# Attention on TensorE: a head's score products are issued one head earlier, and VectorE's softmax is written as two steps

## The reference

```python
def attention(q, k, v):
    s = jnp.einsum('bqhgd,bkhd->bhgqk', q, k, preferred_element_type=jnp.float32) * (HEAD_DIM ** -0.5)
    p = jax.nn.softmax(s, axis=-1).astype(v.dtype)
    return jnp.einsum('bhgqk,bkhd->bqhgd', p, v)
...
    k_all = jnp.concatenate([kc, kl], axis=1)
    v_all = jnp.concatenate([vc, vl], axis=1)
    ol = blocked_attention(ql.reshape(B, T, KV_HEADS, GROUP, HEAD_DIM), k_all, v_all)
    yl = (ol.reshape(B, T, ATT_W) * jax.nn.silu(gl)) @ w_out
```

## Time and profile before

| what | value |
|---|---|
| median of the runs shown (3 runs) | 3914.93 us |
| their lowest and highest | 3911.76 and 3934.26 us |
| the profiled execution: its span | 3915.0 us |
| TensorE busy, share of the span | 92% |
| VectorE, ScalarE, GpSimd | 52%, 39%, 6% |
| mean granted TensorE clock of the core | 0.965 |

### The profile page before, as it was taken

One profiled execution on the slowest core, in us unless ns is written; L12 is line 12 of the kernel. 1 busy time (PEld: TensorE's weight loads), 2 busy tenths in 40 slices (PEclk: granted clock), 3 DMA queues, 4 the chain that ended last, 5 costly groups with the idle time before them and its releaser, 6 DMA issues. The chain is left out here.

```text
span 3915.0 us, 73945 instructions
## 1 busy us (share of the span) xinstructions
PE 3610.4 (92%) x32796; PEld 2969.4 (76%) x32796; DVE 2019.5 (52%) x3476; ACT 1544.0 (39%) x2599; POOL 251.1 (6%) x295
## 2 busy tenths in 40 slices
PE   7899999999899998989988799989999999999998
PEld 3577666767666676777678689847989799999877
DVE  1444454544445457675465646666544455555444
ACT  1333343333333333354454444334443444444433
POOL 0001111110111113002000000100000000000000
PEclk8899899999999998999999899999999999999999
DMA  9423333242343315443324454424554545555554
GB/s 365 145 74 96 89 106 104 81 126 70 94 126 91 100 56 192 170 153 106 97 97 138 154 166 143 138 97 140 172 183 140 169 163 183 183 179 189 194 174 160
DMA packets 349484, 548.76 MB, mean 140 GB/s; under 512 B 11724, under 2 KB 119916, under 8 KB 346988
## 3 DMA queue, kind: packets, MB, share of 16 engines
q1 hardware_dynamic: 346716, 538.78, 42.6%
q10 hardware_dynamic: 2448, 5.24, 0.4%
HBM read 535.86 MB, written 8.13 MB: 139 GB/s over the span
## 5 line engine op out<-in xcount | busy, mean ns | idle before, releaser
L302 PE MATMUL lane<-r,r 128*128 128x256 f32 (+1 forms) x8520 | 1504.7, 325 | 48.4 <-DVE r L260 41.7
L302 PE MATMUL bank<-r,r 128*128 128x512 f32 (+2 forms) x6360 | 1403.0, 359 | 37.6 <-DVE r L260 29.0
L302 PEld LDWEIGHTS lane<-r,r 128*128 128x128 f32 x8520 | 1260.6, 190 | 222.2 <-DVE r L260 48.6
L260 DVE TENSOR_TENSOR r<-ring,r 128x1024 fp32r<-128x1024 f32 x770 | 939.6, 1227 | 940.9 <-ACT r L299 939.6
L302 PEld LDWEIGHTS bank<-r,r 128*128 128x128 f32 x6360 | 1045.0, 193 | 253.5 <-issue 55.3
L299 ACT ACTIVATE r<-ring 128x1024 fp32r<-128x1024 f32 x770 | 807.9, 1055 | 967.5 <-PE lane L302 566.7
L302 PE MATMUL lane<-arena 64*64 64x64 f32 (+5 forms) x13708 | 664.2, 250 | 57.1 <-issue 20.4
L302 PEld LDWEIGHTS lane<-arena 64*64 64x64 f32 (+3 forms) x13708 | 504.9, 140 | 203.3 <-issue 121.4
L299 ACT ACTIVATE arena<-lane 128x256 f32<-128x256 f32 (+3 forms) x578 | 252.6, 457 | 567.0 <-PE lane L302 468.0
L271 DVE COPY arena<-lane 128x256 f32<-128x256 f32 (+3 forms) x366 | 131.7, 361 | 303.5 <-PE lane L302 300.5
L260 DVE TENSOR_TENSOR arena<-arena 128x256 f32<-128x256 f32 (+7 forms) x568 | 259.8, 488 | 36.0 <-ACT arena L299 14.8
(11 more groups left out here) (95 smaller groups left out, 1357.5 us busy)
## 6 DMA issues: line engine op xcount, KB each, us to landing
ring<-in_w_gate_up SPq DMA_DIRECT2D x88, 1024.0 KB, 5.1
ring<-in_mod_w SPq DMA_DIRECT2D x73, 1024.0 KB, 5.3
ring<-in_ev_w_in SPq DMA_DIRECT2D x44, 1024.0 KB, 8.7
ring<-in_w_down SPq DMA_DIRECT2D x44, 1024.0 KB, 5.1
ring<-in_od_w_in SPq DMA_DIRECT2D x40, 1024.0 KB, 5.1
ring<-in_w_in SPq DMA_DIRECT2D x40, 1024.0 KB, 5.1
ring<-in_w_xkv SPq DMA_DIRECT2D x32, 1024.0 KB, 5.2
ring<-in_ev_w_out SPq DMA_DIRECT2D x28, 1024.0 KB, 5.1
```

The lines of the kernel that those rows point to most:

```text
L260: return Nothing() if self.e is None else self.e.tensor_tensor(o, a, b, op)
L302: return Nothing() if self.e is None else self.e.matmul(o, l, r, start=start, stop=stop)
```

## The change

It has three parts. In `attend`, the scores of head h + 1 are issued ahead of the probability transposes of head h, where they were issued after the values of head h; the first head of the stage, and a head whose queries are not transposed yet (head 12), still issue their own. On VectorE, `soft_rows` is taken apart for this attention: the step `scores` does both rows' maxima, and a new step `soften` waits for the exponentials and does both reciprocals and scalings. `soften` of head h + 1 stands behind `p_turned` of head h, mostly with a weight unit between it and the maxima. VectorE's own wait for `pS_read` goes; the one on ScalarE stays.

```diff
+    scored = set()
+
+    def score(h):
+        if h < 16 and h // 4 in ready and h not in scored:
+            scored.add(h)
+            for qt in range(2):
+                step("scores", h // 4, h, qt, bank(aux))
+
+    def soften(h):
+        if h in scored and h not in softened:
+            softened.add(h)
+            step("soften", h)
...
     def attend(n):
         for h in range(4 * n, 4 * n + 4):
-            for qt in range(2):
-                step("scores", n, h, qt, bank(aux))
+            if h not in scored:
+                score(h)
+                yield ATT[0]
+            soften(h)
+            score(h + 1)
             yield ATT[0]
             for kt2 in range(2):
                 step("p_turned", h, kt2, bank(aux))
+            soften(h + 1)
             yield ATT[1]
             step("values", n, h, bank(aux))
             yield ATT[2]
...
     def scores(n, h, qt, b):
         i = (2 * h + qt) % 4
-        if h >= 2:
-            v.wait_ge(*at("pS_read", h - 2))
-        soft_rows(b, 512, M.pS[i], float(P) ** -0.5, M.st1[:, 32 + 4 * i:36 + 4 * i], ("pS", h, qt))
+        st = M.st1[:, 32 + 4 * i:36 + 4 * i]
+        full(b)
+        v.maximum(st[:, 0:1], M.bank[b[0]]).then_inc(*v.n())
+        own()
+        v.ts(st[:, 1:2], st[:, 0:1], -float(P) ** -0.5, None, MUL).then_inc(*v.n(("top", "pS", h, qt)))
+
+    def soften(h):
+        for qt in range(2):
+            i = (2 * h + qt) % 4
+            st = M.st1[:, 32 + 4 * i:36 + 4 * i]
+            v.wait_ge(*at("exp", "pS", h, qt))
+            v.recip(st[:, 3:4], st[:, 2:3]).then_inc(*v.n())
+            own()
+            v.ts(M.pS[i], M.pS[i], st[:, 3:4], None, MUL).then_inc(*v.n(("pS", h, qt)))
```

More of the change, by code:

```diff
@@ L1161, in order_of_work @@
     ready = set()
+    scored = set()
[8 more added lines that the diff above has]
+            step("soften", h)
+    softened = set()
     def attend(n):
         for h in range(4 * n, 4 * n + 4):
-            for qt in range(2):
-                step("scores", n, h, qt, bank(aux))
+            if h not in scored:
[3 more added lines that the diff above has]
+            score(h + 1)
             yield ATT[0]
@@ L3010, in vector_program @@
         read_out, combine, first_done, split_w, split, pool, pool_mix, pool_done, gate_diag, add_first, ctx_done,
-        norm0, norm0_q, h1, h1_done, to_q, to_k, to_v, k_rows, v_rows, q_rows, hn_square, hn_gain, hn_turn, hn_turned, hn_done, scores,
+        norm0, norm0_q, h1, h1_done, to_q, to_k, to_v, k_rows, v_rows, q_rows, hn_square, hn_gain, hn_turn, hn_turned, hn_done, scores, soften,
         values, gate_heads, add_second, attended, norm1, rms, rms_turned, vg_in, gla_ready, gl_gate, gl_decay, gl_spread, gl_keys,
```

## The result

Measured: 3897.43 us in the median (6 runs, 3884.12 to 3903.27) against 3916.14 of the kernel before beside it (6 runs), ratio 0.9945 with a 95% interval from 0.9929 to 0.9961. The change takes 18.7 us away where 10 were forecast. 3897.43 lies in the range, but not in the part of it that carried the forecast (3899 to 3911): it lies where the prediction put the case without a fall of the clock (3890 to 3899).

The account below looks back on a forecast made before the run. TensorE was taken as the bound, with 26 idle us in attention's 223. Idle time falls 13.6 us, less 3.2 for the clock, making 10.4: 3915.0 to 3905 us, range 3896 to 3917 (main case 3899 to 3911).

Parts of the forecast that it names:

- the case without a fall of the clock: Rival: TensorE's clock stays up in attention, giving 3895.5 us; range 3890 to 3899, chance 0.14.
- short waits and `values`, gone: Away from the gate groups, transposes' waits for VectorE's scaling and one `values` wait for ScalarE vanish: 16.8 us saved.
- A: End of gate group 0, with head 10: 5.4 us lost before and after, nothing gained.
- B: End of gate group 1 and head 12: loss goes from 6.1 to 7.5 us, 1.4 worse.
- C: End of gate group 2: no attention step covers the wait, 2.6 us lost becomes 4.1, 1.5 worse.
- clock, before and after: TensorE's granted clock in attention: falls cost 5.9 us before and 9 after, three at 3 each.
- head 0: First head: VectorE still has its scalings ahead of head 1's maxima, costing 0.3 us.
- Part one: Heads away from the gate groups: transposes find their scalings ready, saving 16.8 us together with a wait of `values`.
- Part three: TensorE's clock falls behind three long waits at gate-group ends, 3 us each: 9 against 5.9, 3 us worse.
- The bank coupling: Rival: a head's second transposing waits for the next head's exponentials, 1.9 us to spare; 3925 us, chance 0.07.
- The worse long waits: Rival: at gate-group ends, falls cost 5 us each and another transposing stalls 2; 3913 us, chance 0.16.
- nothing gained: Rival: TensorE's waits count only if units behind can't make up for them; 3915 us, chance 0.05.

Follow-up runs that it names:

- e2: Kernel before with the split softmax alone (both maxima, then both scalings), TensorE's order unchanged: 3893.13 us, ratio 0.9937.
- e3: Changed kernel with 28 extra 128x256 matmuls filling the long wait at the start of gate groups 1 to 3: 3896.49 us, ratio 0.9948.
- e1: Changed kernel with TensorE's new order but VectorE's softmax in one piece as before: 3900.32 us, ratio 0.9961.
- e8: Changed kernel with three extra VectorE reductions ahead of the first maximum at heads 3 to 7 and 9: 3920.24 us, one run.
- e7: Changed kernel with one extra VectorE reduction ahead of the first maximum at heads 3 to 7 and 9: 3895.41 us, one run.
- e9: Kernel of e2 with one extra VectorE reduction ahead of the first maximum at heads 3 to 7 and 9: 3906.99 us, one run.
- e4: Changed kernel with the gate's tiles reordered (four tanh before the high parts, eight products before the low parts): 3886.79 us, ratio 0.9920.
- e5: Kernel of e2 with the gate's tiles reordered as in e4: 3887.02 us, ratio 0.9918.

## Why the prediction was wrong

By the starts on TensorE the losses of the stage are, forecast and measured, in us:

| term | forecast | measured |
|---|---|---|
| short waits and `values`, gone | 16.8 | 15.6 |
| A, idle, before and after | 5.4, 5.4 | 5.4, 4.4 |
| B, the same | 6.1, 7.5 | 6.1, 5.5 |
| C, the same | 2.6, 4.1 | 2.6, 3.5 |
| clock, before and after | 5.9, 9 | 5.7, 4.8 |
| head 0 | +0.3 | 0 |
| sum of the change | -10.4 | -17.2 |

The last line of the measured column is worked out from those above it, 15.6 + 14.1 - 13.4 + 5.7 - 4.8, and comes within 0.3 of the stage's 17.5. The prediction's own sum takes 3.2 for the clock where its terms, 9 less 5.9, give 3.1.

- **Part one, the short waits: right.** They were on the path, they go, nothing takes their place, and head 0 costs nothing (0.3 forecast). The 1.2 us too much are mostly that a wide unit behind scores takes 3.21 us from start to start (1889.66 to 1892.87) and not 2.88, in a quiet order as well. So the 0.48 us that the prediction booked as lost overlap behind each wide unit was mostly the length of the unit itself: what an interruption costs beyond its wait is 0.15 (4.61 less 3.21 less 1.25). What I left out is that the split alone does it too (e2), so the chain that I named as the cause has two ends, and the change cuts both.
- **The places A, B and C: the long waits right, what follows them wrong.** Forecast 4.7, 4.2 and 4.1 lost, measured 4.4, 3.8 and 3.5; at A the release came as forecast, and TensorE was ready at S + 5.33 and not S + 5.0, for the same 3.2 us of the unit behind scores. Then I added 0.7 for `values`, 0.9 for the diagonals and 2.4 for head 12's transposes. The first two aren't there, and the third is 1.6, 1.2 ahead of the transposes and 0.4 within them. These were computed with TensorE at full clock, and the next part put the same stretch at half clock. TensorE can't be slow and also early. e3 shows it: at full clock the waits of `values`, diagonals and transposes appear, 0.51, 0.79 and 1.56 us, and the distance over B stays 11.70 against 11.69.
- **Part three, the failing step: "I take 3 us for each of the three".** The fall comes, and it costs 1.6 each. I took the size from one stretch behind 4.40 us without work at another place of the program and put what follows on top by guess, while three falls that the stage before shows cost 1.7, 2.4 and 1.6. The 9 against 4.8 us are 4.2 of the 7.1 us between forecast and stage; the follow-on waits and the shorter long waits are 3.6 more, part one takes 1.2 back, and 0.5 are small terms. The 5.9 us that the prediction itself had for three falls of today, 2 us each, spoke against the 3.
- **The rivals.** That the clock doesn't fall is refuted as a mechanism, though its 3895.5 lies nearer to the result than my forecast, which is luck: it left out 4.8 us of falls, and had 2.7 us too much in the waits. The bank coupling exists, with the slack that I gave it, and isn't reached: no such wait appears at the heads away from the gate groups. The worse long waits didn't come, and "nothing gained" neither. Of the signs, only one of the three long waits is over 4 us (4.11, 3.27, 3.36), and TensorE's idle time in the stage fell to 11.9 us and not to 17.

The Trainium skill, "TensorE: Matmul & The Clock Gate", section "HAM oscillation — how this bites in real kernels", says that each long enough gap is paid with a cold start; the trace agrees, with half clock behind all three and 1.6 us each. It didn't weigh against the change in the end: ten short waits were worth some 13 us, and of the 4.8 us of the three falls only some 2.3 would have come back with the clock kept up (0.81 at A, nothing at B, 1.52 at C, by e3).

## What to carry to other kernels

Charge a slower clock and the waits behind it once, not twice: lay out the time that each engine arrives with the clock in it, and take the larger. When a consumer waits for a chain that goes back and forth between two engines, first ask whether the chain can be issued in two passes (maxima, then scalings), for that alone gave all of the gain here, and moving the consumer away as well added nothing (2 us less in the stage, nothing that shows in the whole time). A further prize was next door: doing the operations that free a bank ahead of those that don't was worth 7 to 10 us of the stage in every order of the rest, and 2.6 behind it.

## What the runs showed of the hardware

- Over the twelve traces here, TensorE's waits in this stage of 3.2 us and more (17 of them) were followed by a fall to half clock within the next 2 us in 15 cases; two of 3.36 us were not (in e1 and e8). Of 18 waits from 1.9 to 2.7 us, 12 were, and the same length went both ways at the same place of the program: 2.20 and 2.21 us. Of 40 waits from 0.9 to 1.8 us, one was (1.56 in e3). The same page's section "A second HAM failure mode: psum-queue depth-cycling" names short idles between groups as a cause of falls; ten waits of 1.0 to 1.3 us in the kernel before, each with 1.00 behind it, don't bear that out here.
- A fall is short in this stage, and its price varies: 1.6 us each in the changed kernel, 1.7, 2.4 and 1.6 in the kernel before, and 2.3 behind e7's 5.03 us, after which the rows are 0.70 us apart again. Whether one comes behind a wait of about 2 us isn't settled by its length, so the stage of one kernel must be expected to move by some such price from one execution to the next; how often was not measured.
- Time outside the stage differs by up to 11.5 us between profiled executions of kernels that are equal there (e7 and e9), so that a difference of 4.5 us between two of them (e4, e5) is seen in the stage and not in the medians.
